# Norm, turn and split of the first token half in a one-core transformer kernel, in another order

## The chip, the cores and the metric

One core of a Trainium2 chip runs the whole program. The time is device time in microseconds, from one launch; a measurement is the median of some executions. TensorE multiplies matrices, VectorE (DVE) and ScalarE (ACT) work element by element, GpSimd (POOL) too; SyncE (SP) issues most DMAs. Each engine works through its own queue in order, and engines meet in semaphores that the program counts by hand.

## The reference, cut to what matters

Two layers follow one another on x, 1024 tokens by 1024 channels. The stage at issue is the first layer's beginning:

```
h = rms_norm(x, norm1_g[l])
p = h @ w_in[l]
uv = gelu(p[..., :o_s5]);  s_in = p[..., o_s5:o_gate]
br_b = s5_mixer(s_in, lam_re, lam_im, log_dt, b_re, b_im, c_re, c_im, ...)
```

`rms_norm` divides each row by the root of its mean square and multiplies by a gain per channel. The s5 mixer is a linear recurrence over the tokens, with coefficients that are computed from lam, dt, b and c: a table of powers of exp(lam dt), and b and c multiplied by such powers. After this come gates, a spatial gating, an expert layer with top-k routing, and a second layer with attention and a gated recurrence.

## The kernel before, in words

Products are made in float32 quality by splitting each operand into a high part (rounded to a narrower form) and a low part (the rest), and adding three products: high by high, low by high, high by low (`three_passes`, L1416 to L1418).

**The front.** x is loaded as eight row tiles of 128 tokens (`x1[tt]`), four per half h. For a half: the mean squares of its rows (`first_square` on ScalarE, one of them on VectorE, L2620), root and reciprocal (`first_roots`, L2624 to L2629, `norm_scale`), and scaling of the rows on VectorE (`rows_normal`, L2594). TensorE then turns the half so that channels lie on partitions: eight banks ("hT", j), one per channel block k, each made of four 128 by 128 turns, one from each row tile (`turned_x`, L1452). ScalarE makes the high part from a bank and the gain (`hT_high`, L2027), VectorE the low part from bank and high part (`hT_low`, L2602). The first products are the two tiles of s_in (`s_tile`), a pass of 24 products per tile and half: for each k it waits until VectorE has drained bank k. Order on TensorE: turns of the first half, s tiles 0 and 1, turns of the second half, s tiles 0 and 1 again, u tiles, and so on.

**The weight tiles** of s_in (I_S, I_S + 1) are loaded by SyncE between row tiles 3 and 4. Their high parts are made by GpSimd (L1251), their low parts by VectorE (`tile_low`, L2589). Tile I_MERGE's low part (ring_lo) is VectorE's too, made at about 148 us behind the scan.

**The scan's constants.** Small operations of 128 by 16 on VectorE (L2571 to L2581, L2606 to L2642) compute lambda bar and what follows from it; L2667 on, VectorE makes the tables of powers, the low parts of the second half, the tables WR and WI from `s5bc` (b and c, 512 KB), and the scan itself. VectorE's queue runs through all this in program order. `s5bc`, `cols`, `s5d` and the `lncols` are loaded from GpSimd's queue, first thing, and counted on `consts_loaded`.

`step` marks an operation whose end the next one waits for; `xn_ready` counts scaled rows, `squares_done` squares, `full1` filled banks, `front_split` low parts made. VectorE's order in the first half, before:

```
step(stt(tA[:, 0:DM], x1[3], 1.0, x1[3], ALU.mult, ALU.mult, accum_out=ssum[:, 3:4]))
...
step(v.reciprocal(rinv[:, 0:4], root[:, 0:4]))
rows_normal(0)
tile_low(I_S)
dve.wait_ge(consts_loaded, 64)
hT_low(0, 8)
tile_low(I_S + 1)
```

Of the kernel before, what the change touches and what calls it, by code (L numbers as in the profile page):

```python
# [5 lines left out]
F32 = mybir.dt.float32  # L6
F32R = mybir.dt.float32r
U32 = mybir.dt.uint32
ALU = mybir.AluOpType
ACT = mybir.ActivationFunctionType  # L10
AX_X = mybir.AxisListType.X

P = 128
# [378 lines left out]
def build_program(nc, a, out):  # L392
    with ExitStack() as ctx:
# [442 lines left out]
        def high_tile(i):  # L836

            if i < I_V:
                return u_hi[:, i % 2] if i >= I_U else s_hi[:, i]
            if slot_of(i) == 12:  # L840
                return far_a_hi
            return ring_hi[:, slot_of(i)] if slot_of(i) < 8 else far_hi[:, slot_of(i) - 8]
# [378 lines left out]
        def _(pool):  # L1221
# [7 lines left out]
            def split_tiles(first, end):  # L1229

                for i in SPLIT_TILES:
                    if first <= i < end:
# [3 lines left out]
                        else:  # L1236
# [7 lines left out]
            pool.dma_start(s5bc.rearrange("p a b c -> p (a b c)"), a["s5bc"]).then_inc(consts_loaded, 16)  # L1244
# [4 lines left out]
                                    pattern=[[-1, P]], channel_multiplier=1).then_inc(ident_ready, 1)  # L1249
            for i in (I_S, I_S + 1):  # L1250
                nc.gpsimd.tensor_copy(high_tile(i), wait_tile(pool, i)).then_inc(tile_high_ready, 1)  # L1251
            b1.wait_full(pool, ("v", NT - 1))
# [150 lines left out]
        def _(pe):  # L1403
# [40 lines left out]

            def turned_x(first, end):

                for j in range(first, end):
                    h, k = j // 8, j % 8
                    bank = b1.wait_free(pe, ("hT", j))
                    for t in range(4):  # L1450
                        pe.wait_ge(xn_ready, 4 * h + t + 1)
                        last = turn(bank[:, t * P:(t + 1) * P], x1[4 * h + t][:, k * P:(k + 1) * P], ident)  # L1452
                    last.then_inc(full1, 1)
# [18 lines left out]
            turned_x(0, 8)  # L1472
# [144 lines left out]
            pe.wait_ge(upb_loaded, 32)  # L1617
# [361 lines left out]
        def _(act):  # L1979
# [20 lines left out]
            fn(MI[7], MI[4], ACT.Tanh, scale=0.5).then_inc(act_to_s5, 1)  # L2000
            def first_square(tt):

                act.wait_ge(x_moved[tt], 16)
                if tt:
                    act.wait_ge(squares_done, tt)
                fn(junk(0), x1[tt], ACT.Square, accum_out=ssum[:, tt:tt + 1]).then_inc(squares_done, 1)
# [9 lines left out]
            for tt in range(3):  # L2016
                first_square(tt)
            fn(MI[31], MI[3], ACT.Sqrt)
            first_roots(0)
            act.wait_ge(consts_loaded, 64)  # L2020
# [24 lines left out]
            for tt in range(4, NT):  # L2045
                first_square(tt)
            s_there(0, 0)
            first_roots(1)
# [80 lines left out]
            act.wait_ge(upb_loaded, 32)  # L2129
# [418 lines left out]
        def _(dve):  # L2548
# [55 lines left out]

            dve.wait_ge(act_to_s5, 5)
# [13 lines left out]
            dve.wait_ge(x_moved[3], 16)  # L2619
            step(stt(tA[:, 0:DM], x1[3], 1.0, x1[3], ALU.mult, ALU.mult, accum_out=ssum[:, 3:4]))  # L2620
            dve.wait_ge(squares_done, 3)
            dve.sem_inc(squares_done, 1)
            dve.wait_ge(squares_done, 4)
            v.tensor_scalar(msq[:, 0:4], ssum[:, 0:4], 1.0 / DM, EPS, ALU.mult, ALU.add).then_inc(msq_ready, 1)  # L2624
# [3 lines left out]
            dve.wait_ge(root_ready, 1)  # L2628
            step(v.reciprocal(rinv[:, 0:4], root[:, 0:4]))  # L2629
            rows_normal(0)  # L2630
            tile_low(I_S)
            dve.wait_ge(consts_loaded, 64)
            hT_low(0, 8)
            tile_low(I_S + 1)
# [8 lines left out]
            norm_scale(0, 1)  # L2643
            rows_normal(1)
# [31 lines left out]
            hT_low(8, 16)  # L2676
            tile_low(I_U)
            tile_low(I_U + 1)
            complex_multiply(BBR, BBI, s5bc[:, 0], s5bc[:, 1], over(M[20], 16), over(M[21], 16), (16, 16))
# [820 lines left out]
```

## Time and profile before

| | |
|---|---|
| time, three runs | 2770.34, 2770.36 and 2772.02 us; median 2770.36 |
| profiled execution | 2771.3 us, of which the span is 2769.5 us |
| busy, share of the span | TensorE 98%, its weight loads 81%, VectorE 66%, ScalarE 54%, GpSimd 37% |
| chain that ended last | TensorE 88%, VectorE 8%, issue 2%, DMA 1%, ScalarE 1% |
| TensorE in the first of 40 slices (69 us) | 7 tenths busy; from the second to slice 35, 9 tenths |

The span runs from the first to the last instruction; what lies around it is launch and end. Idle time of an engine that is not the one waited for costs nothing, so the shares alone do not say what a change in one stage is worth: who waits for whom in that stage does.

### The profile page before, as it was taken

How to read it: one execution, taken by the hardware profiler on the slowest of the kernel's cores; microseconds unless marked ns; L12 is line 12 of the kernel's file. 1: busy time of each engine (PE TensorE's matmuls, PEld its weight loads, DVE VectorE, ACT ScalarE, POOL GpSimd, SP SyncE). 2: the span in 40 equal slices, each digit the busy share in tenths (PEclk: the TensorE clock that was granted, in tenths of full speed). 3: DMA queues.
4: the chain of work that ended last, by engine and by line, in shares of the span. 5: the costliest groups of instructions: out<-in, count | busy, mean ns of one | idle time of the engine just before them, and what ended most of it. 6: DMA issues, size and time to landing. Idle time of an engine off the chain costs nothing.

```text
span 2769.5 us, 35611 instructions
## 1 busy us (share of the span) xinstructions
PE 2716.3 (98%) x12846; PEld 2234.7 (81%) x12846; DVE 1826.2 (66%) x1987; ACT 1504.1 (54%) x1863; POOL 1034.1 (37%) x506
## 2 busy tenths in 40 slices
PE   7999999999999999999999999999999999998999
PEld 6887888668888888888888887997787888887787
DVE  8972113888888888888888897824454344435662
ACT  5231004467777777777777775327666544443021
POOL 0012222012222222222222232748898855453540
PEclk9999999999999999999999999999999999999999
DMA  5021114499999999999999993522232334338341
GB/s 169 26 75 39 38 54 156 175 392 405 383 383 383 382 383 383 383 383 380 382 383 383 382 349 134 194 74 100 94 117 87 133 109 134 123 118 271 112 182 61
DMA packets 168539, 615.80 MB, mean 222 GB/s; under 512 B 21185, under 2 KB 47825, under 8 KB 135409
## 3 DMA queue, kind: packets, MB, share of 16 engines
q1 hardware_dynamic: 162672, 593.23, 56.9%
q0 software_dynamic: 5328, 20.07, 2.6%
q8 instruction: 68, 1.11, 0.2%
q10 hardware_dynamic: 434, 1.08, 0.1%
q14 instruction: 37, 0.30, 0.0%
HBM read 551.30 MB, written 61.97 MB: 221 GB/s over the span
## 4 chain that ended last, share of the span: by engine, by line
PE 88%; DVE 8%; issue 2%; DMA 1%; ACT 1%; SPq 0%; DVEq 0%; POOLq 0%; ACTq 0%
PE bank L1750 24%; PE bank L1416 19%; PE bank L1418 18%; PE bank L1417 18%; PE bank L1763 2%; PE bank L1896 1%; PE bank L1919 1%; PE bank L1886 1%; DVE buffer L3340 1%; PE bank L1907 1%; PE bank L1813 0%; PE bank L1772 0%; DVE heT_lo L3081 0%; DVE buffer L2759 0%; ACT heT_hi L2304 0%
## 5 line engine op out<-in xcount | busy, mean ns | idle before, releaser
L3031 DVE TENSOR_TENSOR slots_lo<-buffer,slots_hi 128x2048 fp32r<-128x2048 f32 x383 | 849.1, 2283 | 101.0 <-ACT slots_hi L2258 101.0
L2258 ACT ACTIVATE slots_hi<-buffer 128x2048 fp32r<-128x2048 f32 x384 | 708.8, 1950 | 40.7 <-PE bank L1750 25.4
L1300 POOL DMA_INDIRECT xacc<-buffer x15 | 276.5, 18432 | 617.0 <-ACT buffer L2326 617.0
L1341 POOL TENSOR_TENSOR w_lo_set<-buffer,w_hi 128x512 fp32r<-128x512 f32 x210 | 302.2, 1471 | 130.8 <-ACT w_hi L2390 129.2
L1750 PE MATMUL bank<-slots_hi,xsT_hi 128*128 128x512 f32 x960 | 256.9, 390 | 3.4 <-DVE xsT_lo L3049 3.4
L1750 PE MATMUL bank<-slots_lo,xsT_hi 128*128 128x512 f32 x960 | 257.4, 390 | 0.0
L1750 PE MATMUL bank<-slots_hi,xsT_lo 128*128 128x512 f32 x960 | 257.3, 390 | 0.0
L1750 PEld LDWEIGHTS bank<-slots_hi,xsT_hi 128*128 128x128 f32 x960 | 180.2, 188 | 41.2 <-issue 3.6
L1750 PEld LDWEIGHTS bank<-slots_hi,xsT_lo 128*128 128x128 f32 x960 | 180.8, 188 | 37.6
L1750 PEld LDWEIGHTS bank<-slots_lo,xsT_hi 128*128 128x128 f32 x960 | 180.7, 188 | 37.6
L1416 PE MATMUL bank<-slots_hi,heT_hi 128*128 128x512 f32 x512 | 202.5, 395 | 3.1 <-DVE heT_lo L3081 3.1
L1418 PE MATMUL bank<-slots_hi,heT_lo 128*128 128x512 f32 x512 | 199.6, 390 | 0.0
L1417 PE MATMUL bank<-slots_lo,heT_hi 128*128 128x512 f32 x512 | 199.5, 390 | 0.0
L3256 DVE TENSOR_TENSOR buffer<-bank,buffer 128x512 f32<-128x512 f32 x90 | 67.2, 747 | 198.4 <-PE bank L1418 197.8
L1416 PE MATMUL bank<-t_hi,w_hi 128*128 128x512 f32 x480 | 192.0, 400 | 0.0
L1418 PE MATMUL bank<-t_hi,w_lo_set 128*128 128x512 f32 x480 | 187.3, 390 | 0.0
L1417 PE MATMUL bank<-t_lo,w_hi 128*128 128x512 f32 x480 | 187.0, 390 | 0.0
L2390 ACT ACTIVATE w_hi<-buffer 128x512 fp32r<-128x512 f32 x210 | 121.1, 623 | 94.4 <-POOL buffer L1333 76.8
L1416 PE MATMUL bank<-hT_hi,w_hi 128*128 128x512 f32 x360 | 146.2, 406 | 0.0
L1418 PE MATMUL bank<-hT_hi,w_lo_set 128*128 128x512 f32 x360 | 140.3, 390 | 0.0
L1417 PE MATMUL bank<-hT_lo,w_hi 128*128 128x512 f32 x360 | 140.3, 390 | 0.0
L2085 ACT ACTIVATE buffer<-bank,buffer 128x512 f32<-128x512 f32 x32 | 22.1, 690 | 194.7 <-PE bank L1418 194.7
(538 smaller groups left out, 5608.9 us busy)
## 6 DMA issues: line engine op xcount, KB each, us to landing
buffer<-in_w_gate SPq DMA_DIRECT2D x128, 1024.0 KB, 7.8
buffer<-in_w_up SPq DMA_DIRECT2D x128, 1024.0 KB, 4.9
buffer<-in_w_down SPq DMA_DIRECT2D x128, 1024.0 KB, 8.0
buffer<-in_wstream SPq DMA_DIRECT2D x154, 512.0 KB, 4.2
gd<-buffer SPq DMA_DIRECT2D x28, 512.0 KB, 3.9
buffer<-gd SPq DMA_DIRECT2D x20, 512.0 KB, 6.5
buffer<-in_x SPq DMA_DIRECT2D x16, 512.0 KB, 8.3
od<-buffer SPq DMA_DIRECT2D x48, 130.0 KB, 2.0
```

What stands on the lines that cost most here:

```text
L1300: nc.gpsimd.indirect_dma_start(out=xacc, out_offset=bass.IndirectOffsetOnAxis(ap=idx_scatter, axis=0), in_=ys, in_offset=None, compute_op= ...
L1341: nc.gpsimd.tensor_tensor(lo, chunk_raw[p % 2][i], hi.bitcast(F32), ALU.subtract).then_inc(chunk_split.sem, 1)
L1416: mm(bank, lhs[0], rhs[0], start=first, stop=False, skip_group_check=goes_on)
L1417: mm(bank, lhs[0], rhs[1], start=False, stop=False, skip_group_check=goes_on)
L1418: return mm(bank, lhs[1], rhs[0], start=False, stop=last, skip_group_check=goes_on)
L1750: last = mm(psum[first_bank + c][:], x[:, k, :], w_[:, c * HALF:(c + 1) * HALF], start=(k == 0 and x is xsT_hi and w_ is w[0]), stop=(k == ...
L1763: last = mm(psum[4 + c][:], x[:, KD - 1, :], w_[:, c * HALF:(c + 1) * HALF], start=False, stop=x is xsT_lo)
L1886: mm(bank[:], rgig[c][:, j, :], uc[:, h * HALF:(h + 1) * HALF], start=True, stop=True).then_inc(full2, 1)
L2258: fn(slots_hi[:, n_ % NH, :], slots[n_ % NS], ACT.Copy).then_inc(slot_high_ready, 1)
L2390: fn(w_hi[n_ % 8], chunk_raw[p % 2][i], ACT.Copy).then_inc(chunk_high.sem, 1)
L3031: tt2(slots_lo[:, place_of(n_), :], slots[n_ % NS], slots_hi[:, n_ % NH, :].bitcast(F32), ALU.subtract).then_inc(slot_split, 1)
L3256: tt2(dst, y_, x_, ALU.add).then_inc(post_done.sem, 1)
```

## The change: what it does

It touches the first 45 us of the program. On GpSimd: `s5bc` is loaded only after row tile 3 has landed, counted on `upb_loaded`; after the cast of each s tile GpSimd also makes its low part. On TensorE: the first half is turned row tile by row tile, eight turns (one into each bank) as soon as that row tile is scaled. On ScalarE: squares of rows 0, 2, 4, 5 and 6, with scratch areas of their own for neighbouring ones, 4 and 5 ahead of the first `hT_high`, and the load of the root's table ahead of the squares. On VectorE: squares of rows 1, 3 and 7; the order is squares, root and scaling of the first half, its low parts, square 7, scaling of the second half, and then the small operations of the scan's constants that stood around them before; no low parts of the s tiles.

```diff
@@ -1241,14 +1241,18 @@
                                                 ALU.subtract).then_inc(tile_split, 1)
 
             pool.dma_start(cols, a["cols"]).then_inc(consts_loaded, 16)
-            pool.dma_start(s5bc.rearrange("p a b c -> p (a b c)"), a["s5bc"]).then_inc(consts_loaded, 16)
             pool.dma_start(s5d, a["s5d"]).then_inc(consts_loaded, 16)
             pool.dma_start(small[:, 384:392], a["lncols"]).then_inc(consts_loaded, 16)
             step(nc.gpsimd.memset(ident, 0.0))
             nc.gpsimd.affine_select(out=ident, in_=ident, compare_op=ALU.not_equal, fill=1.0, base=0,
                                     pattern=[[-1, P]], channel_multiplier=1).then_inc(ident_ready, 1)
+            pool.wait_ge(x_moved[3], 16)
+            pool.dma_start(s5bc.rearrange("p a b c -> p (a b c)"), a["s5bc"]).then_inc(upb_loaded, 16)
             for i in (I_S, I_S + 1):
                 nc.gpsimd.tensor_copy(high_tile(i), wait_tile(pool, i)).then_inc(tile_high_ready, 1)
+                pool.wait_ge(tile_high_ready, i + 1)
+                nc.gpsimd.tensor_tensor(low_tile(i), raw_tile(i), high_tile(i).bitcast(F32),
+                                        ALU.subtract).then_inc(front_split, 1)
             b1.wait_full(pool, ("v", NT - 1))
             for dst, name in ((wsT, "wsT"), (bsB, "bsB")):
                 pool.dma_start(dst.rearrange("p a b -> p (a b)"), a[name]).then_inc(ln_there, 16)
@@ -1442,6 +1446,15 @@
             pe.wait_ge(ident_ready, 1)
             hT_parts, bra_parts = (hT_hi, hT_lo), (bra_hi, bra_lo)
 
+            def turned_rows():
+
+                for t in range(4):
+                    pe.wait_ge(xn_ready, t + 1)
+                    for k in range(KD):
+                        last = turn(b1.bank(("hT", k))[:, t * P:(t + 1) * P], x1[t][:, k * P:(k + 1) * P], ident)
+                        if t == 3:
+                            last.then_inc(full1, 1)
+
             def turned_x(first, end):
 
                 for j in range(first, end):
@@ -1469,7 +1482,7 @@
                 for h in range(2):
                     split_feature_tile(b1, ("u", 2 * f + h), w, hT_parts, h, KD)
 
-            turned_x(0, 8)
+            turned_rows()
             s_tile(0, 0)
             s_tile(1, 0)
             turned_x(8, 16)
@@ -1614,7 +1627,7 @@
                     last = turn(bank[:, t * P:(t + 1) * P], Yt[:, 4 * jq + t, fh * P:(fh + 1) * P], ident)
                 last.then_inc(full1, 1)
             gates_1("GA", 1)
-            pe.wait_ge(upb_loaded, 32)
+            pe.wait_ge(upb_loaded, 48)
             for j in range(4):
                 b1.wait_drained(pe, ("yT", j))
             for j in range(4):
@@ -1998,12 +2011,14 @@
             act.wait_ge(s5_to_act, 1)
             fn(MI[6], MI[4], ACT.Exp).then_inc(act_to_s5, 1)
             fn(MI[7], MI[4], ACT.Tanh, scale=0.5).then_inc(act_to_s5, 1)
+            first_junk = {0: junk(0), 2: at(30752, DM), 4: at(31776, DM), 5: junk(0), 6: at(30752, DM)}
+
             def first_square(tt):
 
                 act.wait_ge(x_moved[tt], 16)
-                if tt:
-                    act.wait_ge(squares_done, tt)
-                fn(junk(0), x1[tt], ACT.Square, accum_out=ssum[:, tt:tt + 1]).then_inc(squares_done, 1)
+                if tt > 4:
+                    act.wait_ge(squares_done, tt - 4)
+                fn(first_junk[tt], x1[tt], ACT.Square, accum_out=ssum[:, tt:tt + 1]).then_inc(squares_done, 1)
 
             def first_roots(h):
 
@@ -2013,11 +2028,13 @@
             act.wait_ge(s5_to_act, 2)
             fn(MI[10], MI[8], ACT.Sin).then_inc(act_to_s5, 1)
             fn(MI[11], MI[9], ACT.Sin).then_inc(act_to_s5, 1)
-            for tt in range(3):
-                first_square(tt)
             fn(MI[31], MI[3], ACT.Sqrt)
+            first_square(0)
+            first_square(2)
             first_roots(0)
-            act.wait_ge(consts_loaded, 64)
+            first_square(4)
+            first_square(5)
+            act.wait_ge(consts_loaded, 48)
 
             def hT_high(first, end):
 
@@ -2042,10 +2059,9 @@
                 fn(uT[:, j // 2, (j % 2) * HALF:(j % 2 + 1) * HALF], bank[:], ACT.Gelu).then_inc(drained1["act"], 1)
 
             hT_high(0, 8)
-            for tt in range(4, NT):
-                first_square(tt)
+            first_square(6)
+            first_roots(1)
             s_there(0, 0)
-            first_roots(1)
             tile_high(I_U)
             tile_high(I_U + 1)
             s_there(1, 0)
@@ -2126,7 +2142,7 @@
             for k in range(2):
                 act.wait_ge(brB_ready, k + 1)
                 fn(brB_hi[k], brB[:, k, :], ACT.Copy).then_inc(br_high_ready, 1)
-            act.wait_ge(upb_loaded, 32)
+            act.wait_ge(upb_loaded, 48)
             fn(upb_hi.rearrange("p a b -> p (a b)"), upb[:, 0:8].rearrange("p a b -> p (a b)"), ACT.Copy).then_inc(
                 br_high_ready, 1)
             gates_there("GB", 1)
@@ -2602,6 +2618,24 @@
                     stt(hT_lo[:, k, hs], b1.bank(("hT", j))[:], col("norm1", k), hT_hi[:, k, hs].bitcast(F32), ALU.mult,
                         ALU.subtract).then_inc(drained1["dve"], 1)
 
+            def row_squares(tt):
+
+                dve.wait_ge(x_moved[tt], 16)
+                step(stt(tA[:, 0:DM], x1[tt], 1.0, x1[tt], ALU.mult, ALU.mult, accum_out=ssum[:, tt:tt + 1]))
+
+            row_squares(1)
+            row_squares(3)
+            dve.wait_ge(squares_done, 2)
+            dve.sem_inc(squares_done, 2)
+            norm_scale(0, 0)
+            rows_normal(0)
+            dve.wait_ge(consts_loaded, 48)
+            hT_low(0, 8)
+            row_squares(7)
+            dve.wait_ge(squares_done, 7)
+            dve.sem_inc(squares_done, 1)
+            norm_scale(0, 1)
+            rows_normal(1)
             dve.wait_ge(act_to_s5, 5)
             ea, th_, sh, ch = M[6], M[7], M[10], M[11]
             step(stt(M[13], sh, 2.0, ch, ALU.mult, ALU.mult))
@@ -2616,22 +2650,9 @@
             step(tt2(M[20], lim, lim, ALU.mult))
             step(tt2(M[19], M[19], M[20], ALU.add))
             step(v.reciprocal(M[19], M[19]))
-            dve.wait_ge(x_moved[3], 16)
-            step(stt(tA[:, 0:DM], x1[3], 1.0, x1[3], ALU.mult, ALU.mult, accum_out=ssum[:, 3:4]))
-            dve.wait_ge(squares_done, 3)
-            dve.sem_inc(squares_done, 1)
-            dve.wait_ge(squares_done, 4)
-            v.tensor_scalar(msq[:, 0:4], ssum[:, 0:4], 1.0 / DM, EPS, ALU.mult, ALU.add).then_inc(msq_ready, 1)
             step(tt2(M[20], M[16], lre, ALU.mult))
             step(tt2(M[21], M[18], lim, ALU.mult))
             step(tt2(M[20], M[20], M[21], ALU.add))
-            dve.wait_ge(root_ready, 1)
-            step(v.reciprocal(rinv[:, 0:4], root[:, 0:4]))
-            rows_normal(0)
-            tile_low(I_S)
-            dve.wait_ge(consts_loaded, 64)
-            hT_low(0, 8)
-            tile_low(I_S + 1)
             step(tt2(M[20], M[20], M[19], ALU.mult))
             step(tt2(M[21], M[18], lre, ALU.mult))
             step(tt2(M[22], M[16], lim, ALU.mult))
@@ -2640,8 +2661,6 @@
             step(tt2(M[23], ea, ea, ALU.mult))
             step(tt2(M[23], M[23], M[23], ALU.mult))
             step(tt2(r8, M[23], M[23], ALU.mult))
-            norm_scale(0, 1)
-            rows_normal(1)
 
             pR, pI = PW[:, 0], PW[:, 1]
             def complex_multiply(oR, oI, xR, xI, yR, yI, shape):
@@ -2674,8 +2693,10 @@
                                  over(pR[:, :, w_], w_), over(pI[:, :, w_], w_), (16, w_))
 
             hT_low(8, 16)
+            dve.wait_ge(front_split, 2)
             tile_low(I_U)
             tile_low(I_U + 1)
+            dve.wait_ge(upb_loaded, 16)
             complex_multiply(BBR, BBI, s5bc[:, 0], s5bc[:, 1], over(M[20], 16), over(M[21], 16), (16, 16))
 
             for ri in range(2):
```

## Rows read from the trace of the kernel before

**Rows 1.** The page: its span.

```profile
span 2769.5 us, 35611 instructions
```

**Rows 2.** TensorE's timeline: start, us, line, operation, count, idle before and releaser.

```profile
15.49 1.04 PE L1452 MATMUL bank<-buffer 128*128 128x128 f32 x2 [15.49 <-DVE buffer L2594]
...
33.42 3.66 PE L1452 MATMUL bank<-buffer 128*128 128x128 f32 x32
37.91 0.47 PE L1416 MATMUL bank<-hT_hi,s_hi 128*128 128x512 f32 x1 [0.83 <-DVE hT_lo L2602]
...
149.32 0.50 PE L1416 MATMUL bank<-hT_hi,ring_hi 128*128 128x512 f32 x1 [1.71 <-DVE ring_lo L2589]
```

**Rows 3.** Windows: length; busy PE, PEld, DVE, ACT, POOL; clock, DMA share, GB/s.

```profile
4.00:12.00 8.00, 0.00 (x0) 0.00 (x0) 5.23 (x25) 6.59 (x13) 0.28 (x1) 1.00 1.01 395
32.00:148.00 116.00, 114.41 (x631) 95.90 (x630) 111.00 (x190) 29.11 (x44) 0.09 (x1) 1.00 0.17 42
```

**Rows 4.** VectorE's timeline, 0 to 45 us.

```profile
7.37 0.18 DVE L2607 SCALAR_TENSOR_TENSOR buffer<-buffer 128x16 f32<-128x16 f32 x1 [0.39 <-ACT buffer L2015]
...
9.67 0.25 DVE L2618 RECIPROCAL buffer<-buffer 128x16 f32<-128x16 f32 x1
10.77 1.23 DVE L2620 SCALAR_TENSOR_TENSOR buffer<-buffer 128x1024 f32<-128x1024 f32 x1 [0.85 <-DMA buffer<-in_x]
...
12.18 0.90 DVE L2624 TENSOR_SCALAR buffer<-buffer 128x4 f32<-128x4 f32 x1 [0.17 <-DVEq L2622]
...
14.59 2.74 DVE L2594 TENSOR_SCALAR buffer<-buffer 128x1024 f32<-128x1024 f32 x4
17.25 1.22 DVE L2589 TENSOR_TENSOR s_lo<-buffer,s_hi 128x1024 fp32r<-128x1024 f32 x1
18.76 6.00 DVE L2602 SCALAR_TENSOR_TENSOR hT_lo<-bank,buffer,hT_hi 128x512 fp32r<-128x512 f32 x8 [0.30 <-ACT hT_hi L2027]
...
28.60 0.17 DVE L2562 TENSOR_SCALAR buffer<-buffer 128x4 f32<-128x4 f32 x1 [1.16 <-ACT buffer L2006]
...
29.32 2.74 DVE L2594 TENSOR_SCALAR buffer<-buffer 128x1024 f32<-128x1024 f32 x4
32.03 0.07 DVE L2667 MEMSET buffer<- 128x16 f32 x1
...
37.02 5.36 DVE L2602 SCALAR_TENSOR_TENSOR hT_lo<-bank,buffer,hT_hi 128x512 fp32r<-128x512 f32 x8
```

**Rows 5.** DMA issues: KB, us from issue to landing.

```profile
buffer<-in_s5bc POOLq DMA_DIRECT2D x1, 512.0 KB, 7.4
```

**Rows 6.** GpSimd's timeline in the front.

```profile
12.01 1.04 POOL L1251 CAST s_hi<-buffer 128x1024 fp32r<-128x1024 f32 x1 [7.63 <-DMA buffer<-in_wstream]
```

**Rows 7.** ScalarE's timeline in the front.

```profile
9.72 1.06 ACT L2006 ACTIVATE buffer<-buffer 128x1024 f32<-128x1024 f32 x1
...
10.88 1.28 ACT L2018 ACT_TABLE_LOAD   x1
...
17.96 1.48 ACT L2027 ACTIVATE hT_hi<-bank,buffer 128x512 fp32r<-128x512 f32 x2 [4.65 <-PE bank L1452]
```

**Rows 8.** GpSimd's timeline, alone at 203 us and beside VectorE at 2526 us.

```profile
203.54 2.40 POOL L1240 TENSOR_TENSOR ring_lo<-buffer,ring_hi 128x1024 fp32r<-128x1024 f32 x1
...
2526.48 3.33 POOL L1351 TENSOR_TENSOR late_lo<-buffer,late_hi 128x1024 fp32r<-128x1024 f32 x1
2529.73 2.05 POOL L1349 CAST late_hi<-buffer 128x1024 fp32r<-128x1024 f32 x1
```

**Rows 9.** VectorE's timeline at 2526 us.

```profile
2526.33 9.81 DVE L3307 TENSOR_TENSOR yl_lo<-buffer,yl_hi 128x1024 fp32r<-128x1024 f32 x4
```

**Rows 10.** Windows of TensorE alone: length, busy, count, clock, DMA share, GB/s.

```profile
17.39:21.00 3.61, 3.61 (x17) 1.00 1.02 406
22.41:33.42 11.01, 11.01 (x51) 1.00 0.27 97
```

## The prediction

> **What bounds the kernel now.** I read the page first: the span is 2769.5 us [rows 1], and over it TensorE is busy 98% (the table above). A change in the first 40 us can therefore reach the end in one way only: by shifting the moment from which TensorE never waits again. Second, the view of who waits for whom, TensorE alone, over the first 450 us, and TensorE's timeline at the waits it names. The first turn starts at 15.49 us. After it TensorE waits 0.83 us for the low parts of the second half (hT_lo, L2602) and, until 149.32 us, 1.71 us for ring_lo (L2589, the low part of tile I_MERGE) [rows 2]. The reader is to see that both releasers are VectorE and that the later wait is the longer: up to there TensorE has slack and VectorE has none. Third, the windows: from 32 to 148 us VectorE is busy 111.0 of 116 us in 190 instructions [rows 3], and the rest is the 0.03 us that each small dependent operation leaves behind its 0.17 us. So the first half's front is priced by one clock: the time at which VectorE reaches L2667 (the memset that opens the power tables), now 32.03 us [rows 4]. Behind it the change reorders nothing on VectorE, and it adds two waits that are long met. What L2667 loses or gains, the wait at 149 us and the end lose or gain.
>
> **The change part by part, on VectorE's clock.** Up to 6.98 us nothing changes (the row at 7.37 waited 0.39 for the sines) [rows 4].
>
> The constants' load: s5bc (512 KB) goes behind row tile 3. At 395 GB/s [rows 3] it is 1.3 us of transfer, and it took 7.4 us to land beside the row tiles [rows 5]. Row tile 3 landed at 10.7 (VectorE's square began at 10.77) and the first s tile at 12.0 (GpSimd's cast) [rows 4, 6]. The bounds are no gain and 1.3 us; I take 1.3, since both transfers ran in a stretch with the DMA engines at 101%: row tile 3 at 9.4, s tiles at 10.7 and 12.0. s5bc itself is wanted only after the power tables, past 40 us; a landing near 15 us is free. Past it GpSimd's queue holds only the casts, which wait for the s tiles anyway. The waits on upb_loaded and consts_loaded count one DMA more and one less and cost nothing.
>
> The squares: rows 1 and 3 go to VectorE, 1.40 us each (10.77 to 12.18) [rows 4]: row 1 from 7.0 to 8.4, row 3 from 9.4 to 10.8. Behind the wait for row tile 3 stands all of VectorE's queue, and nothing fills the 1.0 us. ScalarE, free at 7.3, loads the root's table (1.28) and takes rows 0 and 2 (1.06 each and the reading of the sum) [rows 7]: done at 11.1. Squares 4 and 5 fit ahead of the first bank. The mean's small operation is issued at about 11.2.
>
> The tile splits: two low parts (1.22 us each on VectorE [rows 4]) go to GpSimd, 2.40 us each when alone [rows 8]. VectorE saves 2.4 us and pays 2.8 us for squares 1 and 7 that it did not have: about +0.4. The larger cost is contention. The small TENSOR_SCALAR at 12.18 took 0.90 us, ending with GpSimd's cast (12.01 plus 1.04) [rows 4, 6]. Near the end the two engines run subtractions side by side: four of VectorE's, without a wait between them, took 9.81 us in place of 4 times 1.22, GpSimd's subtraction 3.33 in place of 2.40 and its cast 2.05 in place of 1.04 [rows 4, 6, 8, 9]. That is strict alternation: each waits out the other's whole instruction. Nothing in the trace shows the scaling of a row (1,024 columns, one input) against GpSimd, so its cost has two ends: no waiting at all, or alternation. I take alternation, by the nearest row (a TENSOR_SCALAR that waited). The chain: cast 10.75 to 11.8; the mean ends with it; root and reciprocal bring row 0's scaling to 12.3 (0.72 from mean to scaling, 28.60 to 29.32 [rows 4], less the mean itself). GpSimd's first subtraction holds 11.9 to 14.3. Then row 0 to 14.9, the second cast to 15.8, row 1 to 16.4, the second subtraction to 18.6, row 2 to 19.2, row 3 to 19.9. I count 0.6 for a row that stands ready and 0.9 and 2.2 for GpSimd's operations that do, since a waiting operation starts some 0.15 sooner. Before, the four rows were done at 17.33.
>
> The Trainium skill bears on the end I take: "SBUF — State Buffer", section "Who interferes with whom", has VectorE and GpSimd share one pair of ports as an exclusive lock in which the later one blocks fully, and counts tensor_scalar among the operations that can take both ports. By that rule the rows alternate, and the time is the forecast; if 1,024-column scalings were exempt, the time would be the first rival's. The 0.90 us row agrees with the rule; no row shows the long form.
>
> The turning: in the old order bank 0 was full four turns after row 3. In the new one every bank fills only with row 3, whose first turn stands behind row 2's eight. In 17.39 to 21 us a turn took 0.212 us (17 in 3.61 [rows 10]), from 33.42 on 0.114 (32 in 3.66 [rows 2]); the windows print a granted clock of 1.00 for the first stretch too, so here the durations, not that column, show the lower of the two levels (1.2 and 2.4 GHz). The eight turns from 19.3 cost 1.7 or 0.9 us, and ScalarE gets its first bank at 21.5 or 20.6. I take the middle, 21.05; before it was 17.96 [rows 7]. The low parts begin 0.80 later and take 0.67 each (5.36 for eight): they end at 27.2. Before: 18.76 plus 6.00, 24.76 [rows 4]. That is 2.4 us late, and VectorE idles about 2 us before them, which the moved small operations used to fill in part.
>
> From there to L2667, before: 7.27 us (24.76 to 32.03: one low part, eight small operations, a wait of 1.16, mean to scaling 0.72, four rows 2.71). After: square 7 (1.40), mean to scaling 0.72, rows 2.71, and 23 small operations, the 12 from 7.37 to 9.9, the three between mean and reciprocal and those eight, at 0.21 (twelve in 2.5 us), 4.83: together 9.66. That is another 2.4 us.
>
> The sum: L2667 at 36.9, so +4.8 us. The profiled execution took 2771.3 and would take 2776.1; the median of three was 2770.36, 0.9 below it, and would be **2775.2 us**. TensorE's first turn comes earlier or equal (about 15.0 against 15.49), but its first product pass is fed at VectorE's pace, and what it has in hand goes into the wait for the second half's low parts, which grows from 0.8 to about 5 us.
>
> **The rivals.**
> *No lock on the rows.* The scalings do not wait: rows from 12.0 to 14.7, turns from 12.7, first bank about 17.4 (squares 4 and 5 hold ScalarE till 17.1), low parts end at 23.6, L2667 at 33.3: +1.2, 2771.6. For it: the only long scalings in the trace ran with GpSimd idle. Against it: the 0.90 us row.
> *The earlier turns reach the end.* If VectorE did not set the end of the front, the first turn at 12.7 in place of 15.49 (that needs no lock either) would give 2.8 us: 2767.6. Against it stands the wait at 149 us [rows 2]: no gain of TensorE's passes it. For it: most of the chain that ended last is TensorE.
> *The clock stays low.* Turns in four bursts with gaps leave TensorE at the lower level through the first product passes: 48 products at 0.46 in place of 0.23 us (the two passes of 24 took 11.0 [rows 10]). With the first at 22.5 they end at 44.4 in place of 33.4, the second half's first low part is ready to be made at about 46 in place of 41.9, and VectorE waits: +9, 2779.4. It decides from about 30 slow products on (7 us in hand, 0.23 each). Against it: the pace of turns doubled within 4 us of steady turning before [rows 10], and the new gaps are short.
>
> **How the numbers follow.** Forecast 0.66 (its own range +3.8 to +6.3, by the two paces of turning and the landings), no lock 0.18, earlier turns 0.06, low clock 0.06, a mixture or something unseen 0.04. The range that leaves out 2 in 10 at most runs from just under the no-lock case to the forecast's slow end with some reserve: 2771.2 to 2777.2. About 0.2% (5.5 us) is what a measurement of this kernel can tell from no change, so the bounds are 2764.8 and 2775.9. Slower than that: a quarter of the forecast (0.17), the low clock and half of the rest, 0.25. Faster needs more than the whole idle time of VectorE's front: 0.02. The same: 0.73.
>
> **What would show it.** Right: on VectorE's timeline the four scalings spread over some 7 us, one or two of them 2 to 3 us long, interleaved with GpSimd's subtractions; the first low part near 22 us; the power tables' first memset near 37; TensorE waiting about 5 us for hT_lo at L1416; the wait at ring_lo still 1 to 2 us. Wrong: the scalings in one block of 2.7 us (no lock); that memset at or before 32 us, or a wait at ring_lo that is gone while the time fell (VectorE did not bound the front); products of 0.46 us after 25 us (low clock).

## The result, and the profile after

The changed kernel takes 2775.51 us in the median (2773.71 to 2777.59, 22 runs), the kernel before 2770.41 (2769.51 to 2773.03, 22 runs): a ratio of 1.0016 with a 95% interval of 1.0010 to 1.0022 (the two medians alone give 1.0018). It is slower by 0.16%, and that is inside the 0.2% that the prediction counted as the same. The profiled execution took 2776.61 us, 5.3 more than the one before; its span stands on the page:

```profile
span 2774.8 us, 35607 instructions
```

VectorE's timeline after, the lines that answer to [rows 4] (start, us, line, operation, count, idle before and its releaser):

```profile
9.67 1.23 DVE L2624 SCALAR_TENSOR_TENSOR buffer<-buffer 128x1024 f32<-128x1024 f32 x1 [1.57 <-DMA buffer<-in_x]
...
11.08 0.91 DVE L2578 TENSOR_SCALAR buffer<-buffer 128x4 f32<-128x4 f32 x1 [0.17 <-DVEq L2629]
12.26 0.18 DVE L2580 RECIPROCAL buffer<-buffer 128x4 f32<-128x4 f32 x1 [0.27 <-ACT buffer L2026]
12.47 7.34 DVE L2610 TENSOR_SCALAR buffer<-buffer 128x1024 f32<-128x1024 f32 x4
22.11 5.36 DVE L2618 SCALAR_TENSOR_TENSOR hT_lo<-bank,buffer,hT_hi 128x512 fp32r<-128x512 f32 x8 [2.29 <-ACT hT_hi L2044]
27.38 1.21 DVE L2624 SCALAR_TENSOR_TENSOR buffer<-buffer 128x1024 f32<-128x1024 f32 x1
...
29.45 2.74 DVE L2610 TENSOR_SCALAR buffer<-buffer 128x1024 f32<-128x1024 f32 x4
...
37.05 0.07 DVE L2686 MEMSET buffer<- 128x16 f32 x1
```

The reader is to see four things. The first half's scalings begin earlier (12.47 for 14.59 us) and last 7.34 in place of 2.74; the second half's four still last 2.74, with GpSimd idle. Then VectorE idles 2.29 us. The low parts end at 27.47 in place of 24.76. From there to the memset that opens the power tables it is 9.58 us in place of 7.27, and the memset comes 5.02 us late. As a sum over that clock: start of the scalings -2.12, their length +4.60, from their end to the first low part 2.30 for 1.43, or +0.87, the low parts 5.36 for 6.00, or -0.64, the rest +2.31; together +5.02.

What stood beside the four scalings, in the view that gives shortest, median and longest duration of a line (ns), and on GpSimd's timeline:

```profile
L2610 DVE TENSOR_SCALAR buffer<-buffer x4: 742/1993/2843, 12.5 to 19.1; 128x1024 f32<-128x1024 f32 x4
```

```profile
10.94 1.03 POOL L1252 CAST s_hi<-buffer 128x1024 fp32r<-128x1024 f32 x1 [0.51 <-DMA buffer<-in_wstream]
12.05 2.34 POOL L1254 TENSOR_TENSOR s_lo<-buffer,s_hi 128x1024 fp32r<-128x1024 f32 x1
14.34 1.49 POOL L1252 CAST s_hi<-buffer 128x1024 fp32r<-128x1024 f32 x1
15.91 2.68 POOL L1254 TENSOR_TENSOR s_lo<-buffer,s_hi 128x1024 fp32r<-128x1024 f32 x1
```

The last row, with nothing on GpSimd any more, took 0.74 us; the longest took 2.84, since it waited out GpSimd's second subtraction (it ended at 18.59) before its own work. GpSimd's second cast and subtraction took 0.46 and 0.34 us longer than its first. TensorE's timeline and its windows (length, busy, count, granted clock, DMA share, GB/s) show what became of it there:

```profile
15.09 3.65 PE L1454 MATMUL bank<-buffer 128*128 128x128 f32 x16 [15.09 <-DVE buffer L2610]
19.20 2.76 PE L1454 MATMUL bank<-buffer 128*128 128x128 f32 x16 [0.47 <-DVE buffer L2610]
23.00 0.47 PE L1420 MATMUL bank<-hT_hi,s_hi 128*128 128x512 f32 x1 [1.04 <-DVE hT_lo L2618]
...
42.90 0.76 PE L1420 MATMUL bank<-hT_hi,s_hi 128*128 128x512 f32 x1 [5.21 <-DVE hT_lo L2618]
...
438.91 0.50 PE L1420 MATMUL bank<-ring_hi,merged_hi 128*128 128x512 f32 x1 [0.92 <-DVE merged_lo L2868]
```

```profile
37.70:42.90 5.20, 0.00 (x1) 0.85 0.00 0
42.90:48.20 5.30, 5.30 (x13) 0.50 0.01 3
48.20:54.00 5.80, 5.80 (x27) 1.00 0.22 90
```

TensorE now waits 5.21 us for the second half's low parts in place of 0.83 [rows 2]. Its granted clock falls while it waits (0.85 in the window of the wait, with no product in it), and it goes on at 0.50, the lower of the two levels, for 5.3 us. The wait at ring_lo, 1.71 us in [rows 2], is gone, but only just. VectorE's timeline has the end of ring_lo, at 154.27 us, and TensorE's the first product that needs it, at 154.32; the product before it began at 154.05, and products follow one another every 0.23 us:

```profile
153.05 1.22 DVE L2605 TENSOR_TENSOR ring_lo<-buffer,ring_hi 128x1024 fp32r<-128x1024 f32 x1
```

```profile
154.05 0.39 PE L1422 MATMUL bank<-ring_hi,hT_lo 128*128 128x512 f32 x1
154.32 0.50 PE L1420 MATMUL bank<-hT_hi,ring_hi 128*128 128x512 f32 x1
```

So VectorE still set the start of this product, by some 0.05 us. A later wait is there in both kernels, for merged_lo, the last place in the first half millisecond where TensorE waits for VectorE. Before it ended so (TensorE's timeline):

```profile
433.93 0.50 PE L1416 MATMUL bank<-ring_hi,merged_hi 128*128 128x512 f32 x1 [0.88 <-DVE merged_lo L2847]
```

This wait does not say which engine bounds the front: it is 0.88 to 0.94 us long in all eleven kernels, and shortly before it VectorE has itself waited for TensorE (VectorE's timeline of the changed kernel):

```profile
427.75 0.69 DVE L2849 TENSOR_TENSOR buffer<-bank,buffer 128x512 f32<-128x512 f32 x1 [23.10 <-PE bank L1422]
```

Its end is only a mark of where TensorE stands behind the front. That end moved by 4.98 us (433.93 to 438.91), the memset by 5.02, the span by 5.3. These two marks, the memset and the end of the wait for merged_lo, are what the experiments are read by: an execution's time varies by some 3 us, the marks of one execution show where a shift was made and whether it was passed on.

### The profile page after: what moved, and what is told of

The parts are those of the page before. It is cut to its first block, busy times and chain, and to the rows that moved or that the text cites. A ratio compares the mean times of both kernels' runs of the same rounds, so it can differ in the third digit from the quotient of the medians.

```text
span 2774.8 us, 35607 instructions
## 1 busy us (share of the span) xinstructions
PE 2722.1 (98%) x12846; PEld 2236.5 (81%) x12846; DVE 1828.6 (66%) x1989; ACT 1501.5 (54%) x1859; POOL 1038.9 (37%) x508
## 4 chain that ended last, share of the span: by engine, by line
PE 93%; DVE 4%; issue 1%; DMA 1%; ACT 1%; SPq 0%; DVEq 0%
PE bank L1763 24%; PE bank L1420 20%; PE bank L1422 20%; PE bank L1421 20%; PE bank L1776 2%; PE bank L1909 1%; PE bank L1932 1%; PE bank L1899 1%; PE bank L1723 1%; PE bank L1920 1%; PE bank L1826 0%; PE bank L1785 0%; DVE buffer L3361 0%; DVE heT_lo L3102 0%; ACT heT_hi L2320 0%
```

## The experiments

The theory: VectorE's clock sets the end, its scalings and GpSimd's operations wait out each other, and the rest of the loss is VectorE's idle time before the first low part, which no small operation fills any more. Rivals: TensorE's side sets the end (its lower clock level, or turns that come late); the loss lies in the squares or loads. Edits are on the changed kernel, except the first.

| kernel | scalings of half 0 | first hT_hi | memset | shift | wait for merged_lo ends | shift | time, ratio to before |
|---|---|---|---|---|---|---|---|
| before | 14.59 to 17.33 | 17.96 | 32.03 | | 433.93 | | |
| changed | 12.47 to 19.81 | 21.30 | 37.05 | +5.02 | 438.91 | +4.98 | 1.0016 [1.0010, 1.0022] |
| low parts alone | 16.59 to 21.27 | 21.90 | 36.73 | +4.70 | 438.64 | +4.71 | 1.0011 [1.0002, 1.0021] |
| subtractions held | 12.18 to 15.48 | 19.12 | 34.86 | +2.83 | 436.74 | +2.81 | 1.0007 [0.9998, 1.0016] |
| turned by bank | 12.04 to 19.37 | 20.00 | 36.46 | +4.43 | 438.34 | +4.41 | 1.0017 [1.0008, 1.0027] |
| both of these | 11.91 to 15.22 | 15.85 | 32.42 | +0.39 | 434.35 | +0.42 | 1.0005 [0.9996, 1.0014] |
| small operations early | 12.09 to 19.42 | 20.87 | 34.27 | +2.24 | 436.19 | +2.26 | 1.0007 [0.9998, 1.0016] |
| constants first | 13.61 to 20.95 | 22.13 | 37.88 | +5.85 | 439.80 | +5.87 | 1.0020 [1.0010, 1.0029] |
| turns twice | 11.71 to 18.93 | 19.63 | 35.38 | +3.35 | 437.31 | +3.38 | 1.0015 [1.0006, 1.0024] |
| turns in the wait | 11.73 to 18.95 | 20.55 | 36.30 | +4.27 | 442.86 | +8.93 | 1.0034 [1.0024, 1.0045] |
| idle time used | 12.65 to 15.95 | 16.58 | 28.48 | -3.55 | 430.43 | -3.50 | 0.9991 [0.9982, 1.0000] |

All columns but the last are starts and ends on the timelines of one execution each. Row tile 3 lands at another time in each (VectorE's square of it starts between 8.79 and 9.87 us where the constants load late), so kernels are best compared from the start of the scalings on.

**The low parts alone**, on the kernel before: nothing else of the change is done.

```diff
             for i in (I_S, I_S + 1):
                 nc.gpsimd.tensor_copy(high_tile(i), wait_tile(pool, i)).then_inc(tile_high_ready, 1)
+                pool.wait_ge(tile_high_ready, i + 1)
+                nc.gpsimd.tensor_tensor(low_tile(i), raw_tile(i), high_tile(i).bitcast(F32),
+                                        ALU.subtract).then_inc(front_split, 1)
...
             rows_normal(0)
-            tile_low(I_S)
             dve.wait_ge(consts_loaded, 64)
             hT_low(0, 8)
-            tile_low(I_S + 1)
```

> The kernel before with one part of the change alone: the two low parts of the s tiles are made by GpSimd right behind their casts, and VectorE makes none; squares, turning order, loads and small operations stay as before. Theory (VectorE and GpSimd wait out each other's whole instructions, and VectorE's clock sets the end): VectorE saves two low parts of 1.22 us, but GpSimd's first subtraction begins at about 13.1, just when the three small operations, then the scalings, are issued; the operations up to the fourth scaling alternate with two subtractions of about 2.4 us and a cast of 1.0, so the scalings end at 20 to 22 in place of 17.33, the first low part of hT begins at 21.5 to 23.5 in place of 18.76, and the memset that opens the power tables comes at 33.0 to 35.0 in place of 32.03 (the wait of 1.16 us for the fourth to seventh squares' mean may go): +1 to +3 us at the wait for merged_lo and in the time (2771.5 to 2774). Rival (the scalings do not wait, and the change's loss lies in squares and order): the memset comes at 29.6 to 31.0, and the time falls by 1 to 2.4 us.

Measured: 2775.45 us against 2772.61. Scalings and first low part (22.70) came where expected, the memset 1.7 us later than the expected range. Its VectorE and GpSimd timelines:

```profile
12.04 0.90 DVE L2627 TENSOR_SCALAR buffer<-buffer 128x4 f32<-128x4 f32 x1 [0.17 <-DVEq L2625]
...
13.05 2.32 DVE L2629 TENSOR_TENSOR buffer<-buffer 128x16 f32<-128x16 f32 x1
15.40 0.94 DVE L2630 TENSOR_TENSOR buffer<-buffer 128x16 f32<-128x16 f32 x1
16.38 0.18 DVE L2632 RECIPROCAL buffer<-buffer 128x4 f32<-128x4 f32 x1
16.59 4.68 DVE L2597 TENSOR_SCALAR buffer<-buffer 128x1024 f32<-128x1024 f32 x4
22.70 6.39 DVE L2605 SCALAR_TENSOR_TENSOR hT_lo<-bank,buffer,hT_hi 128x512 fp32r<-128x512 f32 x8 [1.43 <-ACT hT_hi L2030]
...
33.16 0.17 DVE L2565 TENSOR_SCALAR buffer<-buffer 128x4 f32<-128x4 f32 x1 [2.52 <-ACT buffer L2009]
...
36.73 0.07 DVE L2668 MEMSET buffer<- 128x16 f32 x1
```

```profile
11.88 1.04 POOL L1251 CAST s_hi<-buffer 128x1024 fp32r<-128x1024 f32 x1 [7.50 <-DMA buffer<-in_wstream]
13.00 2.34 POOL L1253 TENSOR_TENSOR s_lo<-buffer,s_hi 128x1024 fp32r<-128x1024 f32 x1
15.28 1.03 POOL L1251 CAST s_hi<-buffer 128x1024 fp32r<-128x1024 f32 x1
16.40 2.34 POOL L1253 TENSOR_TENSOR s_lo<-buffer,s_hi 128x1024 fp32r<-128x1024 f32 x1
```

The alternation can be read off line by line. A 128 by 16 operation that takes 0.17 us alone takes 2.32 beside GpSimd's subtraction and 0.94 beside its cast; both end within 0.1 us of GpSimd's. The scalings end 3.94 us later than before. The part that the expectation missed: in the old order ScalarE's squares 4 to 7 stand behind its eight high parts, so these, 3.94 us late, delay the second mean, and VectorE waits 2.52 us for it in place of 1.16 [rows 4]. This one move, which takes 2.44 us of work off VectorE, costs 4.7 us by itself. That the whole change costs no more than 5.0 means that its other parts, gains and losses, come to some 0.3 together on top of it.

**The subtractions held back** until the rows are scaled: only the contention is taken away.

```diff
                 nc.gpsimd.tensor_copy(high_tile(i), wait_tile(pool, i)).then_inc(tile_high_ready, 1)
+            pool.wait_ge(xn_ready, 4)
+            for i in (I_S, I_S + 1):
                 pool.wait_ge(tile_high_ready, i + 1)
```

> The changed kernel with GpSimd's two subtractions of the s tiles held until all four rows of the first half are scaled (both casts run first). Theory, VectorE's clock and the shared port: the four scalings shrink from 7.3 us to about 3.4 (one cast may still come between), done at 15.9 in place of 19.8; the turns then run at the lower clock level from about 14, so that ScalarE gets its first bank at 18.8 to 19.7 in place of 21.3; the memset that opens the power tables comes at 34.6 to 35.5 in place of 37.05, and the end moves by as much, 1.6 to 2.5 us less than the changed kernel. Rival, the scalings are slow for a reason other than GpSimd's instructions: they stay at 7 us and nothing moves. Rival, TensorE's start sets the end: the end gains no more than the first turn does (under 0.7 us).

Measured: 2773.65 us against 2772.03. VectorE's timeline:

```profile
12.18 3.30 DVE L2612 TENSOR_SCALAR buffer<-buffer 128x1024 f32<-128x1024 f32 x4
19.92 5.36 DVE L2620 SCALAR_TENSOR_TENSOR hT_lo<-bank,buffer,hT_hi 128x512 fp32r<-128x512 f32 x8 [4.44 <-ACT hT_hi L2046]
...
34.86 0.07 DVE L2688 MEMSET buffer<- 128x16 f32 x1
```

The scalings take 3.30 (one of them 1.32 beside the second cast, the others 0.74). That is 4.04 us less, but the memset gains only 1.90 from the scalings' start (24.58 to 22.68). The rest went into a longer wait before the first low part, 4.44 us: TensorE, given rows every 0.74 us, turns 32 blocks without a pause in 6.14 us from 13.64 on and fills its first bank only with the 25th. So alternation, taken away alone, gives back 1.90 us (less than the 2.40 of the small operations below), and the turning order holds back the rest.

**Turned by bank again**, first alone, then with the subtractions held:

```diff
-            turned_rows()
+            turned_x(0, 8)
```

> The changed kernel with the first half turned bank by bank again, as before; all else as changed. Theory (the first bank stands behind eight turns of row 2 at the lower clock level): the first bank is full right after row 3, at 20.4 in place of 21.3, but the banks then follow 0.85 us apart until the clock rises, so the low parts end at 26.8 to 27.4 (27.4 in the changed kernel), the memset comes at 36.5 to 37.1 and the time moves by 0 to -0.5 us. Rival, turning by row tiles is a gain of its own: without it the memset comes at 38 us or later and the time grows by 1 us or more.

> The changed kernel without both suspects: GpSimd's subtractions held until the first half's rows are scaled, and the first half turned bank by bank. Theory: scalings done by 15.5, ScalarE's first bank at 16.1 to 16.5, low parts end at 22.9 to 23.5, then square 7, root, scaling and 23 small operations (9.6 us): the memset at 32.5 to 33.1, so 0.5 to 1.0 us behind the kernel before, and the time 0 to 1.5 us over it. The two gains are not additive with holding the subtractions alone (1.9): together about 4.2. Rival, the first bank is held up by something else (the squares of rows 4 and 5 on ScalarE): first bank at 17.5 or later, memset at 34 or later.

Measured: 2776.77 us alone, 2772.76 with both. Alone it is worth next to nothing (24.58 to 24.42 from the scalings' start): the first high part begins 0.63 us after row 3 in place of 1.49, but the low parts, paced by turns, take 6.08 in place of 5.36. With the subtractions held it is worth 2.2 us more (22.68 to 20.51): three turns, in place of 24, stand before the one that fills the first bank. The two do not add up; held rows only pay if the turns behind them let the first bank through.

**Small operations early**: twelve of the scan's small operations, with their wait for ScalarE, moved back in front of the low parts, where VectorE idles.

```diff
             rows_normal(0)
+            dve.wait_ge(act_to_s5, 5)
+            ea, th_, sh, ch = M[6], M[7], M[10], M[11]
+            step(stt(M[13], sh, 2.0, ch, ALU.mult, ALU.mult))
...
+            step(v.reciprocal(M[19], M[19]))
             dve.wait_ge(consts_loaded, 48)
             hT_low(0, 8)
```

> The changed kernel with the first twelve small operations of the scan's constants put back ahead of the first half's low parts, into the 2.3 us in which VectorE idles there. Theory (VectorE's clock sets the end): the low parts start 0.2 to 0.4 us later, twelve operations of 0.21 us are gone behind them, the memset comes at 34.7 to 34.9 in place of 37.05 and the end is 2.1 to 2.4 us earlier; TensorE's wait for the second half's low parts shrinks from 5.2 to about 3 us. Rival, TensorE's lower clock after that wait sets the end: the gain is larger, 3 us or more, because the shorter wait leaves the clock up. Rival, VectorE does not set the end: no change.

Measured: 2773.91 us. From the scalings' start to the memset 22.18 in place of 24.58: 2.40 us, all but 0.1 of the twelve operations' 2.5. VectorE no longer waits before the low parts. That is the direct proof that the idle 2.29 us was paid later in full.

**Constants first**: s5bc loaded as before, second in GpSimd's queue, nothing else.

```diff
             pool.dma_start(cols, a["cols"]).then_inc(consts_loaded, 16)
+            pool.dma_start(s5bc.rearrange("p a b c -> p (a b c)"), a["s5bc"]).then_inc(upb_loaded, 16)
...
-            pool.wait_ge(x_moved[3], 16)
-            pool.dma_start(s5bc.rearrange("p a b c -> p (a b c)"), a["s5bc"]).then_inc(upb_loaded, 16)
```

> The changed kernel with s5bc loaded second on GpSimd's queue again, as before; all else as changed. Theory: row tile 3 lands 1.1 to 1.3 us later, so VectorE's square of it starts near 10.8 in place of 9.7; the scalings start 1.0 to 1.3 us later, and the memset that opens the power tables comes at 38.0 to 38.4 in place of 37.05, the wait for merged_lo at 439.9 to 440.2 in place of 438.9. Rival, the load is hidden anyway: nothing moves by more than the 0.4 to 0.7 us by which the first transfers differ from run to run.

Measured: 2776.62 us against 2771.78. Row tile 3's square began at 10.82 and the scalings at 13.61, against 9.67 and 12.47: the late load is worth 1.1 us, and 0.8 of it stood at the memset (37.88 against 37.05, just short of the expected 38.0; the second sixteen turns of the first half took 2.46 us here and 2.76 there). The other 1.0 us by which the scalings start earlier than before (13.61 for 14.59) is not of the squares: the mean begins at 12.22 against 12.18 [rows 4]. It comes of the three small operations that no longer stand between mean and reciprocal, one of which had waited beside a cast (VectorE's timeline, of the kernel before and of this one):

```profile
13.39 0.95 DVE L2627 TENSOR_TENSOR buffer<-buffer 128x16 f32<-128x16 f32 x1
```

```profile
12.22 0.90 DVE L2577 TENSOR_SCALAR buffer<-buffer 128x4 f32<-128x4 f32 x1 [0.17 <-DVEq L2628]
13.39 0.18 DVE L2579 RECIPROCAL buffer<-buffer 128x4 f32<-128x4 f32 x1 [0.27 <-ACT buffer L2025]
```

**Turns twice**: each turn of the second half made two times, so that TensorE's wait for hT_lo is filled with work.

```diff
-                    for t in range(4):
+                    for t in (0, 1, 2, 3, 0, 1, 2, 3) if h else range(4):
```

> The changed kernel with each turn of the second half made twice into its bank, so that 3.7 of the 5.2 us that TensorE waits ahead of the third product pass are filled with turns (this is the test that the 44 turns missed: their bank was the one that the pass itself waits for). Theory (TensorE's lower clock level after that wait costs only slack): no lower level near 41 us, the pass's products 0.23 us apart from its start, the wait for ring_lo back at 1.5 to 2 us, and the wait for merged_lo at 438.9 as in the changed kernel (less what the memset is earlier or later in this run). Rival, the lower level is part of the loss: merged_lo's wait 1 to 2.6 us earlier.

Measured: 2774.86 us. Waits of TensorE up to 450 us (engine, line, releaser: us in total, times, longest), and its windows:

```profile
PE bank L1420 <- DVE hT_lo L2618: 2.8, 2, 1.8
PE bank L1420 <- DVE ring_lo L2605: 1.7, 1, 1.7
PE bank L1420 <- DVE merged_lo L2868: 0.9, 1, 0.9
```

```profile
33.00:41.24 8.24, 6.46 (x60) 1.00 0.00 0
41.24:47.00 5.76, 5.76 (x25) 1.00 0.00 0
```

The wait is 1.8 us, the clock stays at its upper level, and the wait at ring_lo is back at 1.7. And the second mark still stands +3.38 behind before, as the memset does (+3.35). So the lower level in the changed kernel used up slack and cost nothing at the end. (The memset is 0.9 us nearer to the scalings' start than in the changed kernel: the second sixteen turns of the first half took 1.97 us here and 2.76 there.)

**Turns in the wait**: 44 more turns before the second half's first products, meant to do the same.

```diff
             turned_x(8, 16)
+            bank = b1.wait_free(pe, ("s", 0, 1))
+            for _ in range(44):
+                turn(bank[:, 0:P], x1[4][:, 0:P], ident)
```

> The changed kernel with 44 turns without use (into the bank that the next pass overwrites) put into TensorE's 5.2 us wait ahead of the second half's first product pass. Theory (VectorE's clock sets the end, and what TensorE's lower clock level costs there is only slack): products from 43 us on start 0.23 us apart in place of 0.43, TensorE reaches its wait for ring_lo about 2.5 us earlier and waits 1.5 to 2.5 us there, and the end stays within 0.4 us of the changed kernel. Rival, the lower level after the long wait is part of the 5 us: the end comes 1 to 2.6 us earlier.

Measured: 2780.68 us. The experiment missed what it was made for. The bank it wrote to is freed only by VectorE's first low part of the second half, so the turns ran behind the wait (TensorE's timeline):

```profile
42.06 7.68 PE L1491 MATMUL bank<-buffer 128*128 128x128 f32 x44 [5.13 <-DVE hT_lo L2621]
49.50 0.47 PE L1420 MATMUL bank<-hT_hi,s_hi 128*128 128x512 f32 x1
```

It shows something else: the added turns put the pass off by 7.44 us (42.06 to 49.50) and moved the second mark by 4.66 more than the memset. TensorE's slack between the two is thus about 2.8 us. The 2.4 us that twelve slow products cost in the changed kernel (0.43 us apart in place of 0.23, from 42.90 to 48.15) fit into that with little to spare, as the 0.05 us left at ring_lo showed; 7.44 us do not.

**The idle time used**: the subtractions held until the first high part is made, banks turned one by one, squares 6 and 7 on ScalarE, and the small operations dealt out to VectorE's waits (7 between squares 1 and 3, 6 behind the first scalings, 10 behind the low parts).

```diff
+            pool.wait_ge(hT_high_ready, 1)
+            for i in (I_S, I_S + 1):
                 pool.wait_ge(tile_high_ready, i + 1)
...
-            turned_rows()
+            turned_x(0, 8)
...
             first_square(6)
+            first_square(7)
             first_roots(1)
```

> A version from the findings: s5bc late and squares shared as changed, GpSimd's subtractions only from the first high part on (VectorE then reads banks and one buffer), turned bank by bank, square 7 on ScalarE, and the 23 small operations spread over VectorE's idle places: seven between its two squares, six behind the scalings, ten behind the low parts. Theory (VectorE's clock): low parts 17 to 23.4, memset at 28.6 to 29.3 in place of 32.03 before and 37.05 changed; the wait for merged_lo 2.5 to 3.3 us before that of the kernel before (433.9); the time 2.5 to 3.3 us under the kernel before, just clear of what the rounds can tell. Rival, TensorE becomes the bound once VectorE is ahead: its third product pass starts near 36 in place of 37.9, so the end gains no more than about 2 us and the wait for ring_lo (1.7 us before) goes under 0.5.

Measured: 2768.86 us, a ratio of 0.9991 with an interval that ends at 1.0. VectorE's timeline, and GpSimd's beside it:

```profile
12.65 3.30 DVE L2613 TENSOR_SCALAR buffer<-buffer 128x1024 f32<-128x1024 f32 x4
...
17.41 5.70 DVE L2621 SCALAR_TENSOR_TENSOR hT_lo<-bank,buffer,hT_hi 128x512 fp32r<-128x512 f32 x8 [0.25 <-ACT hT_hi L2046]
...
28.48 0.07 DVE L2686 MEMSET buffer<- 128x16 f32 x1
```

```profile
17.35 4.73 POOL L1256 TENSOR_TENSOR s_lo<-buffer,s_hi 128x1024 fp32r<-128x1024 f32 x2 [3.93 <-ACT hT_hi L2046]
```

The memset comes 3.55 us before that of the kernel before, and the second mark 3.50 before. From the end of the low parts to the memset it is 5.37 us in place of 9.58: thirteen small operations and square 7 (1.40 us) are gone from there; square 7 was not tried alone. The same two subtractions, made while VectorE makes low parts from banks, take 2.37 us each, as alone [rows 8], and the low parts take 0.71 us apiece, 0.67 in the changed kernel with GpSimd idle. The thought that TensorE might bound the front at this point fell too: it still waits 1.74 us for ring_lo.

## Why the prediction was right

Its steps, with what was measured:

- **The clock that counts.** Right. In nine of the ten kernels the second mark moved with the memset to within 0.05 us, from -3.5 to +5.9; the tenth is the one with work put behind TensorE's wait.
- **The constants' load.** Square 3 began at 9.67 for 9.4 foreseen. Worth 1.1 us for 1.3 taken.
- **The mean blocked by the cast** to 11.8: it ended at 11.99, having taken 0.91 us. Row 0 was foreseen at 12.3 and began at 12.47.
- **Alternation on the rows.** This was the choice between two ends that no row decided. The rows were to end at 19.9 and ended at 19.81. The Trainium skill's "SBUF — State Buffer", section "Who interferes with whom", was the rule weighed there; the trace agrees with it for the long scalings (up to 2.84 us beside a subtraction, 0.74 alone), which no row before had shown. The rival without a lock, 2771.6 us, is out.
- **The turning.** Foreseen: the first bank 0.7 or 1.6 us behind row 3, by the level of the clock, and the middle taken. Measured 1.49 in the changed kernel (first high part at 21.30 for 21.05), 1.60 and 0.70 in two others with the same order up to there. Both ends occur, and what decides between them was not foreseen: that the middle served is luck. In the old order bank 0 was full one turn behind row 3, not four as the prediction has it; its sum took the 17.96 from the row, so nothing hung on that.
- **Low parts to memset.** Foreseen 9.66 us, measured 9.58. The low parts were to end at 27.2 and ended at 27.47; the memset was to come at 36.9 and came at 37.05.
- **TensorE's wait for hT_lo**, about 5 us: 5.21.
- **The wait at ring_lo, still 1 to 2 us: wrong.** It is gone. The prediction took it that after the longer wait TensorE would go on at its old pace. In fact its clock fell to the lower level during that wait, and it lost 2.4 us. The rival on a low clock had looked for that in the first product pass, where it did not happen (the products from 23.00 on follow one another at 0.23 us); it happened two stages later, for 12 products, where the rival wanted 30 to reach the end. Here the prediction was lucky: the loss that it left out used up TensorE's slack to within 0.05 us and no more. That VectorE's clock still counted is shown by the end of ring_lo, and by the run with doubled turns, where the wait at ring_lo is back at 1.7 us and the second mark is still as late as the memset; the wait for merged_lo does not show it.

The sum was +4.8 us at the memset and is +5.02. The profiled execution was to take 2776.1 and took 2776.61; the median 2775.2, and it is 2775.51.

What stays open: the time moves less than the marks in some runs (+2.8 us for +4.7 with the low parts alone, +1.6 for +2.8 with the subtractions held). Single times scatter by 3 us and the intervals are about as wide, so nothing is concluded from that.

## What to carry to other kernels

Work that is moved to an idle engine is paid for on the busy one if the two wait for each other: two subtractions taken off VectorE saved it 2.4 us of work and still made it 4.7 us later, and the same two, put beside operations that did not wait for them, cost nothing. Price a front on the one engine's clock that sets a later wait, operation by operation, idle time included; small operations that look like filler are worth their whole length where they fill a wait. And a mark, the start of one named instruction, shows within one execution to some 0.05 us whether a shift was passed on, where times scatter by 3. Between executions a mark moves too (row tile 3's square began between 8.79 and 9.87 us, and the same sixteen turns took 1.97 to 2.87), so a difference of under 1 us between two kernels is to be looked for row by row.

## What the runs showed of the hardware

- VectorE's scalings, its mean of 128 by 4 (0.17 us became 0.91) and its operations with two inputs from SBUF, even 128 by 16, waited for GpSimd's whole instruction (0.17 us became 2.32), and GpSimd's operations waited in turn for VectorE's rows. VectorE's low parts, which read one input from a bank, and GpSimd's subtractions beside them did not: 0.71 and 2.37 us. Nor did a reciprocal of 128 by 4, which reads SBUF only: at 12.26 us in the changed kernel, inside GpSimd's subtraction from 12.05 on, it took 0.18 us.
- While TensorE waited 5.21, 5.26 and 5.27 us (changed kernel, subtractions held, constants first), after a stretch of products and turns, its granted clock fell from 1.00 to 0.50, so that already the first product behind the wait ran at the lower level; after waits of 2.95, 2.93 and 1.78 us it stayed at 1.00. It is not the length alone: with the small operations early a wait of 2.68 us was followed by three products at the upper level and then by a stretch at 0.50 (window 41.00 to 44.20 us of that kernel):

```profile
41.00:44.20 3.20, 3.20 (x9) 0.50 0.02 5
```

- With the same order of work up to there, sixteen turns of the first half took between 1.97 and 2.87 us in different executions. What decides it was not tried.
